# Feed-forward layers on unnormalised x: the row norm's factor applied to the gate's sum and to the output sum

## What is computed

```python
    merged = g[:, :, 0] * y_attn + g[:, :, 1] * y_conv + g[:, :, 2] * y_pool
    x = x + merged @ w_o[l]

    h = rmsnorm(x, norm_ffn_g[l])
    gt, up = jnp.split(h @ w_ffn_in[l], 2, axis=-1)
    x = x + (jax.nn.silu(gt) * up) @ w_ffn_out[l]
```

## Time and profile before

| | us |
|---|---|
| median of 3 runs | 1573.46 (1570.94 to 1575.38) |
| profiled execution, its time | 1571.23 |
| its span in the profile | 1569.4 |
| PE busy in it | 1524.5 (97%) |
| DVE busy | 1149.5 (73%) |
| ACT busy | 819.5 (52%) |
| POOL busy | 131.5 (8%) |

### The profile page before, as it was taken

How to read it: one execution, slowest core, us unless ns; L and a number is a source line. 1 busy time by engine, 2 the same in 40 slices (tenths; PEclk the granted TensorE clock), 3 DMA queues, 4 the chain that set the end, 5 groups by cost and what they waited for, 6 DMA issues and landing times. The chain is left out here.

```text
span 1569.4 us, 25089 instructions
## 1 busy us (share of the span) xinstructions
PE 1524.5 (97%) x10118; PEld 1342.1 (86%) x10118; DVE 1149.5 (73%) x1497; ACT 819.5 (52%) x1113; POOL 131.5 (8%) x119
## 2 busy tenths in 40 slices
PE   7999999999999999999998989999999999999998
PEld 6999889999799988999987678887888888878887
DVE  6798678786678867878569777777878766766665
ACT  6464454444646445444468755445656565655442
POOL 2060000000113000000004000000111102000000
PEclk9999999999999999999999999999999999999999
DMA  9765366666775646667632247766887765346652
GB/s 327 263 222 202 134 232 229 205 239 240 249 269 202 203 134 232 201 218 274 236 128 96 93 171 269 259 223 193 288 289 251 267 168 187 108 150 211 211 171 102
DMA packets 223762, 327.42 MB, mean 209 GB/s; under 512 B 12216, under 2 KB 175520, under 8 KB 223648
## 3 DMA queue, kind: packets, MB, share of 16 engines
q1 hardware_dynamic: 216584, 315.11, 59.6%
q10 hardware_dynamic: 7064, 10.71, 1.9%
HBM read 316.32 MB, written 9.47 MB: 208 GB/s over the span
## 5 line engine op out<-in xcount | busy, mean ns | idle before, releaser
L1768 DVE TENSOR_TENSOR wparts<-raw,wparts 128x2048 fp32r<-128x2048 f32 (+1 forms) x240 | 545.7, 2279 | 209.7 <-ACT wparts L1285 209.5
L1285 ACT ACTIVATE wparts<-raw 128x2048 fp32r<-128x2048 f32 (+1 forms) x240 | 454.5, 1897 | 118.9 <-PE bank L566 86.3
L564 PE MATMUL bank<-hT,wparts 128*128 128x256 f32 x1216 | 349.1, 287 | 1.7 <-DVE hT L1869 1.5
L565 PE MATMUL bank<-hT,wparts 128*128 128x256 f32 x1216 | 344.3, 283 | 0.0
L566 PE MATMUL bank<-hT,wparts 128*128 128x256 f32 x1216 | 344.3, 283 | 0.0
L564 PEld LDWEIGHTS bank<-hT,wparts 128*128 128x128 f32 x1216 | 233.1, 192 | 6.3 <-issue 6.0
L565 PEld LDWEIGHTS bank<-hT,wparts 128*128 128x128 f32 x1216 | 233.4, 192 | 0.2
L566 PEld LDWEIGHTS bank<-hT,wparts 128*128 128x128 f32 x1216 | 233.3, 192 | 0.0
L564 PE MATMUL bank<-wparts,aT 128*128 128x512 f32 (+1 forms) x536 | 212.8, 397 | 0.7 <-DVE aT L1849 0.5
L565 PE MATMUL bank<-wparts,aT 128*128 128x512 f32 (+1 forms) x536 | 208.0, 388 | 0.0
L566 PE MATMUL bank<-wparts,aT 128*128 128x512 f32 (+1 forms) x536 | 207.7, 388 | 0.0
(11 more groups left out here) (284 smaller groups left out, 1882.3 us busy)
## 6 DMA issues: line engine op xcount, KB each, us to landing
raw<-in_mlp_w SPq DMA_DIRECT2D x64, 1024.0 KB, 5.5
ada_raw<-in_ada_w SPq DMA_DIRECT2D x96, 512.0 KB, 6.4
raw<-in_w_ffn_in SPq DMA_DIRECT2D x44, 1024.0 KB, 5.3
raw<-in_w_in SPq DMA_DIRECT2D x43, 1024.0 KB, 5.7
raw<-in_dil_w_in SPq DMA_DIRECT2D x64, 512.0 KB, 4.9
raw<-in_w_ffn_out SPq DMA_DIRECT2D x22, 1024.0 KB, 5.3
raw<-in_w_o SPq DMA_DIRECT2D x8, 1024.0 KB, 5.0
biasb<-head_bias ACTq DMA_DIRECT2D x16, 512.0 KB, 6.6
```

Of the source, the lines that this page charges most:

```text
L564: pe.matmul(dst, held[:, 0, :], streamed[:, 0, :], start=start, stop=False)
L565: pe.matmul(dst, held[:, 0, :], streamed[:, 1, :], start=False, stop=False)
L1285: act.activation(view(whi[c % SPL], c), view(raw[c % RAW], c), ACT.Copy).then_inc(s_hi, 1)
L1768: dve.tensor_tensor(view(wlo[c % SPL], c), view(raw[c % RAW], c), view(whi[c % SPL], c).bitcast(F32), ALU.subtract).then_inc(s_lo, 1)
```

## The change

In layer l of the first block, with "factor" for the row norm's result:

- `xnf` is gone. PE transposes x itself (`raw_block`): the lower half of the columns in 8 blocks before WO 3, the upper half in 4 blocks after WO 3 (token tile 0) and 4 more amid GT 0 (`upper_blocks`, token tile 1). ACT and DVE write the lower half of `hT` while WO 3 runs.
- GT 0 runs over the lower half of `hT` for both of its column tiles first, then over the upper half (`first_gate`).
- Amid UP 0 PE spreads the factor over the partitions with two matmuls (`spread_rstd`); DVE copies the result into `rstd_rows`.
- In every chunk ACT takes the gate's sum out with Copy, DVE multiplies it in SBUF by `rstd_rows`, ACT applies Silu in place. UP is left unscaled; the factor comes in when DN's sums are added to x.
- The split of WO 1's low part on DVE moves from behind the fourth gated pair to between the third pair's sum and its low part. The split of UP 0 on DVE stands behind `norm_out` and ahead of the two means (before: behind `norm_out` too, but both means stood ahead of `norm_out`). On ACT the split of UP 0 stands between the two halves of `norm_high`.
- SP's wait ahead of the seven bias inputs is for the second factor (`s_rstd`) in place of `s_xn`.

```diff
@@ PE
+                def raw_block(k, t, b=None):
+                    nm = ("nrm", 2 * l + 1, k)
+                    if b is not None:
+                        begin("a", nm, freed_by=(s_hlo, low_done(2 * l + 1, k // 2)), b=b)
+                    return pe.transpose(bank[jobs[nm][2]][:, P * t:P * t + P], x[:, t, P * k:P * k + P], ident[:, :])
+
                 for c in range(4):
...
+                    if c == 3:
+                        for t in range(TT):
+                            emptied(pe, ("WO", l, 0, t))
+                        for k in range(DK // 2):
+                            raw_block(k, 0, turned[k])
+                            end(raw_block(k, 1), ("nrm", 2 * l + 1, k))
                     w = weights(("WO", l, c))
                     wide_half(("WO", l, out_half), ("WO", l, c), w, half, None if out_half else ("mg", l))
-                three_for_weights()
-                norm(2 * l + 1, xnf)
+                emptied(pe, ("WO", l, 1, 0))
+                for k in range(DK // 2, DK):
+                    raw_block(k, 0, (sums[0], sums[1], turned[0], turned[1])[k - DK // 2])
...
+                def upper_blocks():
+                    emptied(pe, ("WO", l, 1, 1))
+                    for k in range(DK // 2, DK):
+                        end(raw_block(k, 1), ("nrm", 2 * l + 1, k))
+
+                def first_gate(name, w):
+                    bk = begin("w", name)
+                    for ks in (range(DK // 2), range(DK // 2, DK)):
+                        for i in range(2):
+                            for k in ks:
+                                await_pair(("nrm", 2 * l + 1), i, k)
+                                m = mm3(bk[:, S * i:S * i + S], w[:, :, k, P * i:P * i + P], hT[:, :, k, :],
+                                        (i, k) == (0, 0), (i, k) == (1, DK - 1))
+                            if (i, k) == (0, DK // 2 - 1):
+                                upper_blocks()
+                    end(m, name)
+
+                def spread_rstd():
+                    at = RSTD_OF[2 * l + 1]
+                    pe.wait_ge(s_rstd, at + 2)
+                    bk = begin("a", ("rstd", l))
+                    for t in range(TT):
+                        m = pe.matmul(bk[:, P * t:P * t + P], rstd[:, (at + t) % 2, 0:1].broadcast_to([P, P]), ident[:, :],
+                                      start=True, stop=True)
+                    end(m, ("rstd", l))
...
@@ SP
                 if name[0] == "UP" and name[2] == 0:
                     l = name[1]
-                    sp.wait_ge(s_xn, 2 * (2 * l + 1) + 2)
+                    sp.wait_ge(s_rstd, RSTD_OF[2 * l + 1] + 2)
...
@@ ACT
-                for c in range(4):
+                for c in range(3):
                     split_ahead(("WO", l, c))
-                norm_sums(2 * l + 1, sqf)
-                norm_upper(2 * l + 1, xnf)
-                norm_high(2 * l + 1, lambda k: colA[:, c_ffn(l) + k:c_ffn(l) + k + 1])
+                out_square(0, 0)
+                out_square(0, 1)
+                norm_high(2 * l + 1, ffn_gain, range(DK // 2))
+                split_ahead(("WO", l, 3))
+                out_square(1, 0)
+                norm_high(2 * l + 1, ffn_gain, range(DK // 2, DK))
+                out_square(1, 1)
...
-                        act.activation(sg[c % 2][:, :, :], bk[:, :].rearrange("p (a s) -> p a s", a=2), ACT.Silu)\
+                        act.activation(sg[c % 2][:, :, :], bk[:, :].rearrange("p (a s) -> p a s", a=2), ACT.Copy)\
                            .then_inc(drain_sem(("GT", l, c)), 1)
                         split_ahead(("UP", l, c))
                         stage_biases(u0)
+                        act.wait_ge(s_scaledgate, NF1 * l + c + 1)
+                        act.activation(sg[c % 2][:, :, :], sg[c % 2][:, :, :], ACT.Silu).then_inc(s_silu, 1)
...
@@ DVE
                     gated("YA", 0, jp).then_inc(s_mg, 1)
+                    if jp == 2:
+                        split_ahead(("AO", l, 1))
                     h_low(mg[:, 2 * jp:2 * jp + 2, :], hT_lo[:, 2 * jp:2 * jp + 2, :], hT_hi[:, 2 * jp:2 * jp + 2, :], 0.5)
-                split_ahead(("AO", l, 1))
...
                     half = c - 1
+                    if half:
+                        norm_out(2 * l + 1, ffn_gain, (0, 1))
                     for t in range(TT):
...
                         dve.tensor_tensor(xs, xs, bk[:, :], ALU.add).then_inc(drain_sem(nm), 1)
-                        if (half, t) == (1, 0):
-                            norm_mean(2 * l + 1, 0)
-                norm(2 * l + 1, xnf)
-                norm_out(2 * l + 1, lambda k: colA[:, c_ffn(l) + k:c_ffn(l) + k + 1])
+                norm_out(2 * l + 1, ffn_gain, (2, 3))
+                split_ahead(("WO", l, 3))
+                for t in range(TT):
+                    norm_mean(2 * l + 1, t)
...
                         split_ahead(("UP", l, c))
+                        if c == 0:
+                            bk = full(dve, ("rstd", l))
+                            dve.tensor_copy(rstd_rows[:, :], bk[:, 0:S]).then_inc(drain_sem(("rstd", l)), 1)
+                            emptied(dve, ("rstd", l))
+                        emptied(dve, ("GT", l, c))
+                        dve.tensor_tensor(sg[c % 2][:, :, :], sg[c % 2][:, :, :],
+                                          rstd_rows[:, :].unsqueeze(1).broadcast_to([P, 2, S]), ALU.mult).then_inc(s_scaledgate, 1)
                         steps_of(u0 + 3)
-                        emptied(dve, ("GT", l, c))
+                        dve.wait_ge(s_silu, NF1 * l + c + 1)
...
-                    dve.tensor_tensor(xs, xs, bk[:, :], ALU.add).then_inc(drain_sem(nm), 1)
+                    dve.scalar_tensor_tensor(out=xs, in0=bk[:, :], scalar=rstd[:, (RSTD_OF[2 * l + 1] + t) % 2, 0:1], in1=xs,
+                                             op0=ALU.mult, op1=ALU.add).then_inc(drain_sem(nm), 1)
```

More of the change, by code:

```diff
@@ L184, in block_pair @@
             sqf = sb("sqf", [P, D], at=ph)
-            xnf = sb("xnf", [P, TT, D], at=ph)
+            rstd_rows = sb("rstd_rows", [P, S], at=ph)
             sg = [sb(f"sg{i}", [P, 2, S], at=ph) for i in range(2)]
@@ L382, in block_pair @@
         RSTD_OF = (0, 6, 8, 14, 16, 28, 30, 56)
-        TURN_EARLY = {e: (0, 1, 2, 3, 4, 5, 6, 7) if e == 0 else (0, 1, 3, 4, 5, 6, 7) if e in (1, 3) else
-                      (0, 1, 2, 3, 4, 5, 6) if e == 5 else (0, 3, 4, 5) if e == 7 else (0, 1, 2, 3, 4, 5) for e in range(8)}
+        TURNED_AT = {0: 0, 2: 1, 4: 2, 5: 3, 6: 4, 7: 5}
+        TURN_EARLY = {e: (0, 1, 2, 3, 4, 5, 6, 7) if e == 0 else (0, 1, 2, 3, 4, 5, 6) if e == 5 else (0, 3, 4, 5) if e == 7 else (0, 1, 2, 3, 4, 5) for e in range(8)}
         def low_done(e, kp):
@@ L636, in choose_slab_banks @@
             def choose_slab_banks():
-                slab_banks[:] = [(n["w"] + i) % WB for i in range(WB)] + [(n["a"] + 4) % AB + WB]
+                slab_banks[:] = [rings["w"][(n["w"] + i) % WB] for i in range(WB)] + [rings["a"][(n["a"] + 4) % AB]]
                 slabs_begun[0] = 0
@@ new lines, in _ @@
+                n.update(w=0, a=0)
+                accs = None
+                def upper_blocks():
[13 more added lines that the diff above has]
+                    end(m, name)
@@ L830, in _ @@
                             w = weights((nm, l, c))
-                            feature_major((nm, l, c), w, (0, P), hT, 0, DK,
-                                          first_of=None if c or i else ("nrm", 2 * l + 1))
+                            if c or i:
+                                feature_major((nm, l, c), w, (0, P), hT, 0, DK, between=idle if c else spread_rstd)
+                            else:
+                                first_gate((nm, l, c), w)
                             used((nm, l, c))
@@ L1334, in h_high, with norm_high @@
                 act.activation(dst, src, ACT.Copy, scale=scale).then_inc(s_hhi, 1)
-            def norm_high(e, gain):
-                for k in range(DK):
+            def norm_high(e, gain, ks=range(DK)):
+                for k in ks:
                     if (e, k) == (0, 2):
@@ L1858, in split_half, with norm_out @@
                                   view(whi[0], 0)[:, rows, :].bitcast(F32), ALU.subtract).then_inc((s_half[2], s_lo)[half], 1)
-            def norm_out(ev, gain):
-                for kp in range(DK // 2):
+            def norm_out(ev, gain, kps=range(DK // 2)):
+                for kp in kps:
                     if (ev, kp) == (0, 1):
```

26 lines of the change are left out of this document (17 added, 9 removed).

## The result

| | us |
|---|---|
| kernel before, median of 5 | 1573.46 (1570.94 to 1575.38) |
| changed kernel, median of 5 | 1585.42 (1582.81 to 1586.55) |
| ratio | 1.0073 (95%: 1.006 to 1.0085) |
| profiled execution, its time and span | 1582.81, 1580.8 |

The ratio is estimated over all runs and differs a little from the quotient of the medians, 1.0076. The page hardly shows it: PE's busy time has grown by 2.2 us on the earlier trace rows, the span by 11.4.

What follows compares the result with a forecast made beforehand. The prediction took the moment of SP's release, which GT 1's load waits for, to decide the time: 7.2 us lost in layer 0 plus 7.1 in layer 1, 14.3 on the 1573.46 median, gives 1587.8 us; range 1580 to 1594.

Steps and rivals of the forecast that it cites:

- What bounds it: In each layer the first gate chunk, GT 1, hangs on when SP is released, though PE is busy 97%.
- SP's release: Ahead of the seven small loads, layer 0: SP goes on at 205.2 instead of 199.85, 5.4 us later.
- PE's own gains: Before GT 1, layer 0: PE arrives at 210.5 instead of 213.78, gaining 3.2 us, 1.15 of it at WO 1.
- The landing of GT 1's load: From issue to ACT, layer 0: 5.87 us as before, so GT 1's split ends at 218.2.
- The second rival: SP's release 1 us off and GT 1's landing 1 to 1.5 off, each layer: 1583; chance 0.13.
- The scaling in the first chunk: Between GT 1's split and the product freeing UP 0's bank: copy, scaling and Silu add 1.8 us (1.4 to 2.5).
- The table load: Ahead of the first Silu, 1.28 us: does not stand behind the wait, so costed at nothing.
- the third rival: Table load exposed in each layer, behind the wait for the scaled gate: 2.6 us more, 1590.4; chance 0.12.
- The other ten chunks: Behind the first chunk: DVE's extra 0.65 us per chunk is hidden, and PE gives back nothing of the loss.
- the fourth rival: DVE becomes the bound of the first two chunks, 2 to 4 us in each layer: 1594; chance 0.07.
- Layer 1: Same chain in the second layer: UP 1 at 619.0 against 611.9, 7.1 us late.
- The first rival: Gain arrives, each layer 3.2 us shorter, 1567.1, if SP is released by 197.55; chance 0.05.

Runs made afterwards that it cites:

- e1: Changed kernel with SP's wait and the seven bias inputs moved from behind UP 0's load to behind UP 1's load; 1571.58 us, ratio 0.9993.
- e5: Kernel before with SP's wait released by DVE's split of UP 0 in place of the last `xnf`; 1585.59 us, ratio 1.0080.
- e4: Kernel before with only DVE's split of WO 1's low part moved between the third pair's sum and its low part; 1569.81 us, ratio 0.9984.
- e2: e1 with DVE's preparation of distances also moved from chunk 0 to chunk 1; 1566.93 us, ratio 0.9965.
- e12: e2 with DVE beginning GT 1's split only when POOL's second power is done; 1566.62 us, ratio 0.9955.
- e8: Changed kernel with the gate's scaling left out, so ACT takes the sum out with Silu (result not the block's); 1582.98 us, ratio 1.0062.
- e11: Changed kernel with 54 spare matmuls on PE filling the gap ahead of GT 1; 1586.08 us, ratio 1.0078.
- e7: Kernel before with SP's wait and the seven bias inputs moved behind UP 1's load; 1571.44 us, ratio 0.9991.
- e9: Changed kernel with DVE's means ahead of UP 0's split, and that split held until the second power is done; 1580.90 us, ratio 1.0047.
- e6: Changed kernel with DVE's two means moved ahead of its split of UP 0; 1585.73 us, ratio 1.0077.
- e10: e2 with PE's small sum of the step heights moved from behind UP 0 to behind GT 1; 1569.73 us, ratio 0.9975.

## Why the prediction was right, and where its sizes were off

*What bounds it.* Right. The forecast rested on SP's release and not on PE's 97%, and e1 and e5 show it from both sides: the release taken off the path gives the 12 us back, the late release alone makes them.

*PE's own gains.* Right in kind and a little small. The gap ahead of WO 1 went (e4 alone: 1.27, where I had 1.15). GT 0's first product at 196.81 and PE's arrival at GT 1 at 209.9 are some 0.5 and 0.6 ahead of my working. I took 0.15 for a transpose; counted from start to start, eight of them held up WO 3 by 0.79 and four held up GT 0 by 0.36, 0.09 to 0.10 each. I also let GT 0's second half begin at 201.1, where my own terms give 200.8. In e2 and e12 these gains come to the end.

*SP's release.* This and the landing are the terms that were mis-sized. I had 205.2, it was 204.52. The order of steps was as worked out (low parts, split, means, powers); DVE's low parts ended at 200.87 instead of 201.4, for PE's sooner arrival, and the powers took 1.09 as a pair. Term: +4.6 instead of +5.4.

*The landing of GT 1's load.* I kept 5.87 us; it was 5.22 in layer 0 (207.37 to 212.59) and 5.50 in layer 1 against 5.27. The second rival had both in it, each some 1 us. In layer 0 the two misses together are 1.4 us, out of 7.2; in layer 1 the release was 0.8 short and the landing 0.2 over the 5.27 that I kept.

*The scaling in the first chunk.* +1.82 measured (8.94 against 7.12), 1.8 forecast: copy 0.41, scaling 0.69, Silu with its hand-overs 0.69. The sum for layer 0 then closes: 4.60 for the release, less 0.65 for the landing, plus 1.82, is 5.77, and UP 1 in fact starts 5.76 later. Taken out alone, scaling and Silu did not give back their share, though: e8 got 0.8 and 1.1.

*The table load.* Right, the third rival falls: it began at 218.82, while its activation waited until 224.41 for the scaled gate.

*The other ten chunks.* Right, the fourth rival falls: the stretch between is not longer, and its 1.2 us less are within what this stretch varies from run to run.

*Layer 1.* I had 7.1 for UP 1; it was 6.5 (61.21 us from the split of WO 0 against 54.72 in the kernel before, where UP 1 started at 611.99), and DN 0 was another 0.4 late, half of it waiting for its split.

*The sum.* 5.76 + 6.91 is 12.7 in the stretches, 11.4 in the span (the stretch between is 1.2 shorter) and 12.0 in the medians; 14.3 was forecast. The range held. Of the 1.6 by which the stretches fall short, 1.4 is layer 0's release and landing.

*The first rival, the gain arriving.* Its deciding point was stated rightly as SP's release. What I had not seen is that the release can be stepped round: the seven loads need not stand ahead of GT 1's.

*Not in the list at all:* the half clock behind the gap. It cost nothing here (e11), but it would have been the answer to "why did e8 bring so little", and a forecast that removes a term behind a 7-us gap must reckon with it. It can also strike in stages that nobody edited (e7's layer 1).

## What to carry to other kernels

When a wait in a DMA queue is given a new releaser, work out when that releaser fires in the new order, and count every load that stands behind the wait: here a release 4.6 us later in each of two layers, with 1.8 us of new gate steps behind it, turned a kernel that can be some 6 us faster (e2) into one 12 us slower. Put inputs that are wanted late behind the loads that are wanted soon, and move their first user with them, but no further than the next user allows. A small operation on POOL that releases others is best done while DVE has no large two-operand instruction running (e9 against e6: SP's release 1.7 us sooner for 0.93 us of waiting on DVE).

## What the runs showed of the hardware that was not expected

- TensorE was granted 0.50 at the start of GT 1 after idle stretches of 7.01, 7.26, 5.01 and 4.24 us (changed kernel and e5), and of UP 1 after 3.05 us (e11, layer 1); with products in the gap it kept 1.00 (e11). After 3.02 us in layer 0 of the same run it kept 1.00.
- The fall can come when PE is at work again: in e9 GT 1 began at 1.00 behind a gap of 3.44 us and fell to 0.50 some 1.2 us later.
- The same stage of the same program does not always get the same clock. The 5.3 us between WO 3 and GT 0, which hold 16 transposes, passed at 1.00 in both layers of the kernel before, but in layer 1 of e7 the clock was at 0.50 from 591.6 to 594.6, across the last transposes and the start of GT 0, which cost 0.7 us.
- Two POOL operations on 128x1 took 2.82 us beside DVE's 128x2048 two-operand split and 1.09 without it (e1, e2, e6 and e10 against the changed kernel, e9 and e12). That a lock on shared ports is the cause was not measured directly; the second power's length and e9 agree with it, while the split itself was not lengthened.
- The table load does not stand behind the semaphore wait of its own activation: it began 5.59 us before it, as soon as ACT's split ended, while the scaled gate was ready only at 224.37.
